# Receptance without the meta tokens, and a first chunk that reads nothing

## The chip, the core and the metric

The program runs on one core of a Trainium2 chip. The metric is the device time of one execution in microseconds (us). Three executions of the kernel before took 1640.95, 1644.88 and 1644.90 us, median 1644.88. The core's engines are TensorE (PE in the profile, PEld for its weight loads), VectorE (DVE), ScalarE (ACT), GpSimd (POOL) and SyncE (SP, which here only issues transfers). They run their own instruction streams and meet at semaphores.

## What is computed

A block of two layers on 16 meta tokens followed by 512 tokens, 1024 features wide. Layer 0 is an attention layer with its feed-forward part, layer 1 an RWKV-7 layer with its own. The output drops the meta tokens. The part that matters here is the recurrence of layer 1:

```python
xs = h[None] + xx[None] * mu[:, None, None, :]
rkv = jnp.einsum('nbtd,nde->nbte', xs[:3], w_rkv)
r, k, v = rkv[0], rkv[1], rkv[2]
...
def step(S, inp):
    r_t, w_t, k_t, v_t, a_t, b_t = inp
    sa = jnp.einsum('bhij,bhj->bhi', S, a_t)
    S = (S * w_t[:, :, None, :] + sa[..., None] * b_t[:, :, None, :]
         + v_t[..., None] * k_t[:, :, None, :])
    return S, jnp.einsum('bhij,bhj->bhi', S, r_t)
...
S0 = jnp.zeros((B, N_HEADS, HEAD_DIM, HEAD_DIM), jnp.float32)
_, y = lax.scan(step, S0, seq_in)
...
bonus = jnp.sum(r_h * k_h * r_k.astype(jnp.float32), axis=-1, keepdims=True) * v_h
...
return rms_norm(h[:, N_META:], final_norm)
```

The receptance r enters nothing but the outputs y and the bonus of its own token. After layer 1 no token looks at another, so y of a meta token reaches no output.

## The kernel before

All large products are in a split form: weight and input are each a high and a low part, and a product is three matmuls (high by high, high by low, low by high; types fp32r). One *unit* is a block of 128 output features. Its weights come by one transfer into w_raw, ScalarE writes w_hi (L125), VectorE writes w_lo (L129), TensorE multiplies, and ScalarE or VectorE evicts. There are two buffers of each kind and two pairs of PSUM banks, used in turn.

The function Front computes the inputs of the recurrence in 32 units. Its tensor() runs them in a written order; each of the 8 receptance units R_UNITS (23, 25 to 31) has 8 row tiles, each in two column halves of 264 (spans, L1914, row_products, L1922), 48 matmuls on line L1928. Between the last five units spread() (L1976, matmuls on L1984) sends the key norms back to all partitions two heads' tiles at a time. VectorE scales the keys with them (L1743, L1747), GpSimd multiplies (L1903), and at the end forms the first chunk's bk (L1909, L1910). evict() (L1552) copies a receptance unit of 528 columns into r.rr on ScalarE. A pad of 48 zero columns ahead makes 576 columns.

chunk_stage then runs the recurrence in 9 chunks of 64 columns over 16 heads; chunk 0 holds the pad and the 16 meta tokens. It is a block of its own: every engine ends Front before any begins it. A step for c does two things interwoven: the *preparation* of chunk n = c + 1 and the *chain* of chunk c. The first step (c = -1) only prepares chunk 0, the second (c = 0) chains chunk 0 and prepares chunk 1. Preparation: l_products (L2437 to L2443), transposes of bk and v (L2452, L2462), a triangular inverse by doubling (times_x L2510, x_times L2529 and L2538, with VectorE between each pair at L2316, L2329, L2339; three levels for chunk 0, five for the others), the quarter products quads (L2476: bk by the pair a, r, 128 stationary by 128 moving columns), which VectorE masks into akm (keys, L2354) and arm (reads, L2358), and a_v (L2488). Chain: w_product (state by a, L2550, woven into the first times_x), chain_u (L2558), y_state_product (state by r, L2563, woven into the second times_x), chain_y (L2569), chain_s (the new state) and the gate's product. products() on VectorE (L2290, L2291) makes ar, and on GpSimd (L2267, L2268) bk of the next chunk; l_products waits for both. bk has one buffer, so GpSimd waits until the quads of the chunk before are done.

The two places where an order is written that matters below:

## Time and profile before

| what | value |
|---|---|
| median of 3 executions | 1644.88 us (1640.95, 1644.88, 1644.90) |
| span of the profiled execution | 1638.5 us |
| TensorE busy | 1567.2 us, 96% of the span |
| VectorE, ScalarE, GpSimd busy | 852.3, 637.0, 156.7 us |
| mean granted TensorE clock | 0.983 |
| the chain that ended last | TensorE on L785 and L1248, 25% of the span |

The profiled execution has no time of its own in the measurements shown, only its span from the first to the last instruction. The median lies 6.4 us above it, which holds what is around the span and the difference between executions. In the profile a matmul's duration is its way through the array, and neighbours overlap, so the pace is read from start to start, not from the duration. A product of fp32 operands (all of chunk_stage but the gate) shows as two matmul records.

### The profile page before, as it was taken

How to read it: one execution, taken by the hardware profiler on the slowest of the kernel's cores; microseconds unless marked ns; L12 is line 12 of the kernel's file. 1: busy time of each engine (PE TensorE's matmuls, PEld its weight loads, DVE VectorE, ACT ScalarE, POOL GpSimd, SP SyncE). 2: the span in 40 equal slices, each digit the busy share in tenths (PEclk: the TensorE clock that was granted, in tenths of full speed). 3: DMA queues.
4: the chain of work that ended last, by engine and by line, in shares of the span. 5: the costliest groups of instructions: out<-in, count | busy, mean ns of one | idle time of the engine just before them, and what ended most of it. 6: DMA issues, size and time to landing. Idle time of an engine off the chain costs nothing. (4 is left out here: it accounts for less than half of the span.)

```text
span 1638.5 us, 35327 instructions
## 1 busy us (share of the span) xinstructions
PE 1567.2 (96%) x15881; PEld 1410.4 (86%) x15881; DVE 852.3 (52%) x1201; ACT 637.0 (39%) x880; POOL 156.7 (10%) x180
## 2 busy tenths in 40 slices
PE   6999998999999999999999989999789999999997
PEld 5998987999999999989988978888558888888886
DVE  5675665544433444677566545545485444344432
ACT  3654654332212223455566333333244322122322
POOL 3100100001000015000000411101010010001100
PEclk9999999999999999998999989999999999999999
DMA  4112121333332333662222100000303333233331
GB/s 132 53 59 72 53 72 46 91 91 90 105 89 78 91 90 115 176 183 71 62 72 59 39 19 4 4 4 5 106 28 98 94 91 114 81 90 102 100 94 64
DMA packets 225814, 126.41 MB, mean 77 GB/s; under 512 B 8856, under 2 KB 220976, under 8 KB 225408
## 3 DMA queue, kind: packets, MB, share of 16 engines
q1 hardware_dynamic: 225360, 124.07, 25.6%
q8 instruction: 125, 2.05, 0.5%
q14 instruction: 25, 0.20, 0.0%
q10 hardware_dynamic: 304, 0.08, 0.0%
HBM read 117.71 MB, written 6.42 MB: 76 GB/s over the span
## 5 line engine op out<-in xcount | busy, mean ns | idle before, releaser
L125 ACT ACTIVATE w_hi<-w_raw 128x1024 fp32r<-128x1024 f32 (+1 forms) x200 | 224.3, 1122 | 548.0 <-PE psg L785 305.8
L785 PE MATMUL psg<-x_hi,w_hi 128*128 128x264 f32 (+1 forms) x1080 | 350.2, 324 | 1.8 <-DVE w_lo L129 1.8
L785 PE MATMUL psg<-x_lo,w_hi 128*128 128x264 f32 (+1 forms) x1080 | 350.4, 324 | 0.0
L785 PE MATMUL psg<-x_hi,w_lo 128*128 128x264 f32 (+1 forms) x1080 | 349.6, 324 | 0.0
L129 DVE TENSOR_TENSOR w_lo<-w_raw,w_hi 128x1024 fp32r<-128x1024 f32 (+1 forms) x200 | 261.9, 1310 | 139.8 <-ACT w_hi L125 139.6
L785 PEld LDWEIGHTS psg<-x_hi,w_hi 128*128 128x128 f32 x1080 | 202.8, 188 | 20.1 <-DVE w_lo L129 2.2
L785 PEld LDWEIGHTS psg<-x_lo,w_hi 128*128 128x128 f32 x1080 | 202.8, 188 | 17.4 <-issue 0.2
L785 PEld LDWEIGHTS psg<-x_hi,w_lo 128*128 128x128 f32 x1080 | 203.3, 188 | 16.7
L1248 PE MATMUL psg<-mid_hi,w_hi 128*128 128x264 f32 (+1 forms) x528 | 170.8, 323 | 2.5 <-DVE w_lo L129 2.5
L1248 PE MATMUL psg<-mid_lo,w_hi 128*128 128x264 f32 (+1 forms) x528 | 170.0, 322 | 0.0
L1248 PE MATMUL psg<-mid_hi,w_lo 128*128 128x264 f32 (+1 forms) x528 | 169.4, 321 | 0.0
L1928 PE MATMUL psg<-x_hi,w_hi 128*128 128x264 f32 x400 | 119.0, 298 | 4.6 <-DVE w_lo L129 2.5
L1928 PE MATMUL psg<-x_lo,w_hi 128*128 128x264 f32 x400 | 116.4, 291 | 0.0
L1928 PE MATMUL psg<-x_hi,w_lo 128*128 128x264 f32 x400 | 116.2, 291 | 0.0
L1172 POOL TENSOR_TENSOR mid_lo<-up,mid_hi 128x528 fp32r<-128x528 f32 (+1 forms) x40 | 52.6, 1315 | 657.7 <-ACT mid_hi L908 657.7
L1248 PEld LDWEIGHTS psg<-mid_hi,w_hi 128*128 128x128 f32 x528 | 99.2, 188 | 11.6 <-DVE w_lo L129 3.6
L1248 PEld LDWEIGHTS psg<-mid_lo,w_hi 128*128 128x128 f32 x528 | 99.2, 188 | 7.8
L1248 PEld LDWEIGHTS psg<-mid_hi,w_lo 128*128 128x128 f32 x528 | 99.3, 188 | 7.6
L958 DVE TENSOR_TENSOR res<-res,psg 128x512 f32<-128x512 f32 (+1 forms) x38 | 26.4, 694 | 143.5 <-PE psg L1248 116.9
L1005 DVE TENSOR_TENSOR gate<-psg,rstd 128x528 f32<-128x528 f32 (+1 forms) x44 | 30.8, 700 | 122.3 <-PE psg L785 115.3
L1015 DVE TENSOR_TENSOR up<-psg,rstd 128x528 f32<-128x528 f32 (+1 forms) x44 | 30.8, 700 | 111.7 <-PE psg L785 111.7
L1928 PEld LDWEIGHTS psg<-x_hi,w_hi 128*128 128x128 f32 x400 | 78.1, 195 | 10.3 <-issue 5.7
(389 smaller groups left out, 3182.7 us busy)
## 6 DMA issues: line engine op xcount, KB each, us to landing
w_raw<-in_w_ffn_in_dram SPq DMA_DIRECT2D x88, 512.0 KB, 3.8
w_raw<-in_w_ffn_out_dram SPq DMA_DIRECT2D x40, 704.0 KB, 4.6
w_raw<-in_w_qkv_dram SPq DMA_DIRECT2D x24, 512.0 KB, 3.8
w_raw<-in_w_rkv_dram SPq DMA_DIRECT2D x24, 512.0 KB, 4.1
w_raw<-in_w_o_attn_dram SPq DMA_DIRECT2D x8, 512.0 KB, 4.1
w_raw<-in_w_o_rwkv_dram SPq DMA_DIRECT2D x8, 512.0 KB, 4.2
v_first<-v_pair SPq DMA_DIRECT2D x8, 264.0 KB, 2.0
res_kept<-res SPq DMA_DIRECT2D x1, 2112.0 KB, 7.8
```

The lines of the kernel that those rows point to most:

```text
L125: k.nc.scalar.activation(k.w_hi[j][:, 0:kt, :], k.raw[j][:, 0:kt, :], ACT.Copy).then_inc(k.hi_ready[j].h, 1)
L129: k.nc.vector.tensor_tensor(k.w_lo[j][:, 0:kt, :], k.raw[j][:, 0:kt, :], k.w_hi[j][:, 0:kt, :].bitcast(F32), ALU.subtract).then_inc(k.lo_r ...
L785: done = k.nc.tensor.matmul(k.psg[:, 2 * j + c, 0:size], w[:, t, :], x, start=t == first and n == 0, stop=t == last and n == 2)
L958: nc.vector.tensor_tensor(row, row, self.psum(i % 2), ALU.add).then_inc(self.freed(i), 1)
L1005: nc.vector.tensor_tensor(self.cols(b.gate), self.psum(0), self.cols(k.rstd), ALU.mult)\
L1015: nc.vector.tensor_tensor(self.cols(b.up), self.psum(1), self.cols(k.rstd), ALU.mult)\
L1172: nc.gpsimd.tensor_tensor(b.mid_lo[:, r, self.t0:T], b.up[:, self.t0:T], b.mid_hi[:, r, self.t0:T].bitcast(F32), ALU.subtract).then_inc(se ...
L1248: done = k.nc.tensor.matmul(self.bank(i, c), w[:, t, :], x, start=t == 0 and n == 0, stop=t == count - 1 and n == 2)
L1928: done = nc.tensor.matmul(k.psg[:, 2 * j + c, 0:size], w[:, t, :], x[:, at:at + size], start=t == 0 and a == 0, stop=t == KT - 1 and a == 2)
```

## The change

Receptance is computed for the 512 tokens alone, so a receptance unit is one piece of 512 columns in one PSUM bank (24 matmuls in place of 48) and is evicted as 512 columns into r.rr from column 64 on. The reads of chunk 0 are left out: no product of ar by r, no arm, no y_state_product, no chain_y, no copy of y; and, since the state is zero there, no w_product: wt is minus av. Chunk 0's quarter products have 64 moving columns (a alone) in place of 128. Semaphore counts shift with it: arm_r now counts chunk 0's keys, y_d, w_d, y_r and ar_r start one chunk later, and chain_s waits for u itself in chunk 0.

```diff
+    def spans(self, n):
+        return [(META, SEQ)] if n >= MIX_R else [(0, HALF), (HALF, HALF)]
...
+        def r_evict(m):
+            i = R_UNITS[m]
+            self.wait_done(act, i)
+            nc.scalar.activation(r.rr[:, m, C:TP], k.psg[:, 2 * ((self.u0 + i) % 2), :], ACT.Copy)\
+                .then_inc(self.freed(i), 1)
...
-        evict(r.rr, R_UNITS, 0)
+        r_evict(0)
...
-        for t in (r.gs, r.aa, r.rr, r.vv, r.kk_in):
+        for t in (r.gs, r.aa, r.vv, r.kk_in):
...
-            at, size = spans[c]
+            at, size = self.spans(n)[c]
...
         def unit(i, first):
             begin(i)
-            for c in range(2):
+            for c in range(len(self.spans(first))):
                 for t in range(KT):
                     row_products(i, first + t, c)
...
                     if chain:
-                        act.wait_ge(y_d.h, c + 1)
-                        nc.scalar.activation(chunk(r.xn, c), wy_ps, ACT.Copy).then_inc(y_r.h, 1)
+                        if c:
+                            act.wait_ge(y_d.h, c)
+                            nc.scalar.activation(chunk(r.xn, c), wy_ps, ACT.Copy).then_inc(y_r.h, 1)
...
                     else:
                         nc.vector.tensor_tensor(ar[p][:, :, 0, :], chunk(r.xn, n), ch.w_ext[:, :, 0:C], ALU.mult)
-                    nc.vector.tensor_tensor(ar[p][:, :, 1, :], chunk(r.rr, n), ch.w_ext[:, :, 1:C + 1],
-                                            ALU.mult).then_inc(ar_r.h, 1)
+                        nc.vector.tensor_tensor(ar[p][:, :, 1, :], chunk(r.rr, n), ch.w_ext[:, :, 1:C + 1],
+                                                ALU.mult).then_inc(ar_r.h, 1)
...
                 def keys(n, half):
                     dve.wait_ge(quad.h, 2 * n + half + 1)
-                    nc.vector.tensor_tensor(akm[C:P, :, :].rearrange("p (b m) c -> p b m c", b=2)[:, :, pairs(half), :],
+                    done = nc.vector.tensor_tensor(akm[C:P, :, :].rearrange("p (b m) c -> p b m c", b=2)[:, :, pairs(half), :],
...
+                    if n == 0:
+                        done.then_inc(arm_r.h, 1)
                 def reads(n, p, half):
+                    if n == 0:
+                        return
...
+                        if c:
+                            dve.wait_ge(w_d.h, c)
+                            nc.vector.scalar_tensor_tensor(wt[:], wy_ps, -1.0, av[q][:], ALU.mult, ALU.subtract)\
+                                .then_inc(wt_r.h, 1)
+                        else:
+                            nc.vector.tensor_scalar(wt[:], av[q][:], -1.0, None, ALU.mult).then_inc(wt_r.h, 1)
...
+                    size = P if n else C
                     for h, m, rows in heads[first:first + len(parts) * KT // 2]:
-                        last = mm(pair_ps[:, h % 2, (m % 4) * P:(m % 4) * P + P],
+                        last = mm(pair_ps[:, h % 2, (m % 4) * P:(m % 4) * P + size],
                                   bk[rows, m, :, :].rearrange("p a c -> p (a c)"),
-                                  ar[p][rows, m, :, :].rearrange("p a c -> p (a c)"), start=True, stop=True)
+                                  ar[p][rows, m, :, :].rearrange("p a c -> p (a c)")[:, 0:size], start=True, stop=True)
...
                 def chain_s(c, q):
+                    if c == 0:
+                        pe.wait_ge(u_r.h, 1)
...
-                    w = (lambda m, rows: w_product(c, q, m, rows)) if chain else None
-                    y_state = (lambda m, rows: y_state_product(c, q, m, rows)) if chain else None
+                    w = (lambda m, rows: w_product(c, q, m, rows)) if c > 0 else None
+                    y_state = (lambda m, rows: y_state_product(c, q, m, rows)) if c > 0 else None
...
-                    if chain:
+                    if c > 0:
                         chain_y(c, q)
```

TensorE at the last spread, in Front, before the change (psg: the unit's sums; psx: the spread):

```order
L1928 MATMUL psg<-x_lo,w_hi0 128x264
L1928 MATMUL psg<-x_hi,w_lo0 128x264
L1984 MATMUL psx<-key_norm_91,put_92 128x264 x4
L1928 MATMUL psg<-x_hi,w_hi1 128x264
L1928 MATMUL psg<-x_lo,w_hi1 128x264
L1928 MATMUL psg<-x_hi,w_lo1 128x264
```

and with it:

```order
L1936 MATMUL psg<-x_lo,w_hi0 128x512
L1936 MATMUL psg<-x_hi,w_lo0 128x512
L1992 MATMUL psx<-key_norm_91,put_92 128x264 x4
L1936 MATMUL psg<-x_hi,w_hi1 128x512
L1936 MATMUL psg<-x_lo,w_hi1 128x512
L1936 MATMUL psg<-x_hi,w_lo1 128x512
```

The spread stands at the same place between two units; the unit behind it has 24 rows of 512 columns in place of 48 of 264.

VectorE in the step that prepares chunk 0, from the first half's keys (akm) on, before (ar1 is chunk 1's, arm0 chunk 0's, g2_lo the gate weight's low part):

```order
L2354 TENSOR_TENSOR akm_10962<-psx,strict 64x2x256
L2316 TENSOR_TENSOR w_raw1<-psg,cross2 128x32x8
L2358 TENSOR_TENSOR arm0_10954<-psx,incl 128x2x256
L2290 TENSOR_TENSOR ar1_10949<-xn_80,w_ext_83 128x8x64
L2291 TENSOR_TENSOR ar1_10949<-rr_79,w_ext_83 128x8x64
L2329 TENSOR_TENSOR xt0_10956<-xt0_10956,psg 128x32x8
L2354 TENSOR_TENSOR akm_10962<-psx,strict 64x2x256
L2358 TENSOR_TENSOR arm0_10954<-psx,incl 128x2x256
L2365 TENSOR_TENSOR g2_lo_99<-g2_raw_98,g2_hi_100 80x2048
```

and with the change:

```order
L2363 TENSOR_TENSOR akm_10769<-psx,strict 64x2x256
L2325 TENSOR_TENSOR w_raw1<-psg,cross2 128x32x8
L2299 TENSOR_TENSOR ar1_10756<-xn_80,w_ext_83 128x8x64
L2300 TENSOR_TENSOR ar1_10756<-rr_79,w_ext_83 128x8x64
L2338 TENSOR_TENSOR xt0_10763<-xt0_10763,psg 128x32x8
L2363 TENSOR_TENSOR akm_10769<-psx,strict 64x2x256
L2378 TENSOR_TENSOR g2_lo_99<-g2_raw_98,g2_hi_100 80x2048
```

Both maskings of arm0 are gone, and all behind them moves up.

TensorE in the step that chains chunk 0, behind the first half of chunk 1's quads, before (xt1 and xs belong to chunk 1's inverse):

```order
L2529 MATMUL psg<-w_raw0,xs_10964 64x32 x2
L2476 MATMUL psx<-ar1_10949,bk_85 128x128 x4
L2510 MATMUL psg<-xt1_10957,low_10963 64x32 x16
L2569 MATMUL psg<-arm0_10954,uv0_10952 64x64 x16
L2529 MATMUL psg<-w_raw1,xs_10964 64x32 x2
L2538 MATMUL psg<-xs_10964,w_raw1 64x32 x2
```

and with the change:

```order
L2545 MATMUL psg<-w_raw0,xs_10771 64x32 x2
L2492 MATMUL psx<-ar1_10756,bk_85 128x128 x4
L2526 MATMUL psg<-xt1_10764,low_10770 64x32 x16
L2545 MATMUL psg<-w_raw1,xs_10771 64x32 x2
L2554 MATMUL psg<-xs_10771,w_raw1 64x32 x2
```

Between times_x and the x_times that needs VectorE's answer to it, chain_y no longer stands.

## Rows read from the trace of the kernel before

**Rows 1.** the page, part 4: the chain that ended last, by engine

```profile
PE 27%; DVE 1%; ACT 0%; issue 0%; DVEq 0%; ACTq 0%
```

**Rows 2.** windows, Front's end, chunk stage: PE, PEld, DVE, ACT, POOL busy, PEclk, DMA

```profile
873.50:942.00 68.50, 66.74 (x469) 62.00 (x468) 34.72 (x34) 29.14 (x38) 16.75 (x10) 0.95 0.16 47
942.00:1130.00 188.00, 170.24 (x5673) 152.66 (x5676) 94.98 (x197) 63.92 (x107) 23.00 (x21) 0.97 0.03 7
```

**Rows 3.** windows of plain products, TensorE alone: 264 columns, then 512

```profile
340.00:440.00 100.00, 100.00 (x824) 1.00 0.32 92
1284.00:1400.00 116.00, 116.00 (x502) 1.00 0.35 101
```

**Rows 4.** timeline of TensorE, last receptance unit: start, us, engine, line

```profile
933.09 2.04 PE L1984 MATMUL psx<-key_norm,put 16*128 16x264 f32 x8
...
935.28 0.28 PE L1928 MATMUL psg<-x_lo,w_hi 128*128 128x264 f32 x1
...
940.91 0.28 PE L1928 MATMUL psg<-x_hi,w_lo 128*128 128x264 f32 x1
...
942.30 0.25 PE L2437 MATMUL psx<-ar,bk 64*64 64x32 f32 x2 [1.11 <-PEq L1255]
```

**Rows 5.** timelines of ScalarE and GpSimd at that unit

```profile
941.23 0.61 ACT L1552 ACTIVATE rr<-psg 128x528 f32<-128x528 f32 x1 [6.59 <-PE psg L1928]
...
935.12 3.47 POOL L1903 TENSOR_TENSOR aa<-aa,xn 128x528 f32<-128x528 f32 x2 [4.56 <-DVE xn L1743]
...
940.25 1.27 POOL L1910 TENSOR_TENSOR bk<-kk_in,w_inv 128x512 f32<-128x512 f32 x1
```

**Rows 6.** timeline of TensorE preparing chunk 0, to chunk 1's l_products

```profile
950.48 1.12 PE L2510 MATMUL psg<-xt,low 64*64 64x32 f32 x32 [0.64 <-DVE xt L2329]
951.53 0.71 PE L2476 MATMUL psx<-ar,bk 64*128 64x128 f32 x8
...
956.75 1.16 PE L2476 MATMUL psx<-ar,bk 64*128 64x128 f32 x16
959.51 1.15 PE L2488 MATMUL psg<-uv,akm 64*64 64x64 f32 x32 [1.59 <-DVE arm L2358]
...
962.78 0.32 PE L2437 MATMUL psx<-ar,bk 64*64 64x32 f32 x2 [2.13 <-issue]
```

**Rows 7.** timelines of VectorE and GpSimd there, GpSimd's last row a chunk later

```profile
958.67 0.69 DVE L2358 TENSOR_TENSOR arm<-psx,incl 128x512 f32<-128x512 f32 x1
959.28 2.28 DVE L2365 TENSOR_TENSOR g_lo<-g_raw,g_hi 80x2048 fp32r<-80x2048 f32 x1
...
958.08 1.27 POOL L2267 TENSOR_TENSOR bk<-aa,w_inv 128x512 f32<-128x512 f32 x1 [12.53 <-PE psx L2476]
959.30 3.38 POOL L2268 TENSOR_TENSOR bk<-kk_in,w_inv 128x512 f32<-128x512 f32 x1
...
985.82 1.28 POOL L2268 TENSOR_TENSOR bk<-kk_in,w_inv 128x512 f32<-128x512 f32 x1
```

**Rows 8.** timelines, chaining chunk 0: TensorE, VectorE; last, TensorE's next chain_y

```profile
972.43 0.47 PE L2563 MATMUL psg<-ar,state 64*64 64x64 f32 x3
...
973.70 0.71 PE L2476 MATMUL psx<-ar,bk 64*128 64x128 f32 x8
...
978.30 1.91 PE L2569 MATMUL psg<-arm,uv 128*64 128x64 f32 x32
980.14 0.32 PE L2529 MATMUL psg<-w_raw,xs 64*64 64x32 f32 x2
...
978.40 0.42 DVE L2316 TENSOR_TENSOR w_raw<-psg,cross 128x256 f32<-128x256 f32 x1 [0.25 <-PE psg L2510]
...
1003.55 1.15 PE L2569 MATMUL psg<-arm,uv 128*64 128x64 f32 x32
```

**Rows 9.** windows of low granted clock in the first chunks, TensorE

```profile
961.60:968.40 6.80, 5.62 (x112) 0.52 0.01 2
978.70:982.10 3.40, 3.40 (x95) 0.54 0.00 0
```

More of the change, by code:

```diff
@@ L1684, in scalar @@
         nc.scalar.activation(r.ghid_hi[:], r.ghid[:], ACT.Copy).then_inc(self.gh_hi.h, 1)
-        evict(r.rr, R_UNITS, 1)
+        r_evict(1)
         self.weights_hi(act, 28)
-        evict(r.rr, R_UNITS, 2)
+        r_evict(2)
         key_scale(2)
@@ L1690, in scalar @@
         self.weights_hi(act, 29)
-        evict(r.rr, R_UNITS, 3)
+        r_evict(3)
         key_scale(4)
@@ L1694, in scalar @@
         self.weights_hi(act, 30)
-        evict(r.rr, R_UNITS, 4)
+        r_evict(4)
         key_scale(6)
@@ L1703, in scalar @@
         nc.scalar.activation(r.ch.w_inv[:], r.gs[:, :, 0:C], ACT.Exp, scale=-DECAY).then_inc(r.ch.exps.h, 1)
-        evict(r.rr, R_UNITS, 5)
-        evict(r.rr, R_UNITS, 6)
-        evict(r.rr, R_UNITS, 7)
+        r_evict(5)
+        r_evict(6)
+        r_evict(7)
     def vector(self, dve):
@@ L1811, in vector @@
         self.weights_lo(dve, 17)
-        dve.wait_ge(self.pads_r.h, 6)
+        dve.wait_ge(self.pads_r.h, 5)
         running(0)
@@ L1859, in vector @@
         dve.wait_ge(r.ch.exps.h, 1)
-        dve.wait_ge(self.pads_r.h, 7)
+        dve.wait_ge(self.pads_r.h, 6)
         dve.wait_ge(self.kk_r.h, 2 * KT)
@@ L1913, in tensor @@
         k, r, nc = self.k, self.r, self.k.nc
-        spans = [(0, HALF), (HALF, HALF)]
         def begin(i):
@@ L1929, in row_products @@
                                         start=t == 0 and a == 0, stop=t == KT - 1 and a == 2)
-            if t == KT - 1 and c == 1:
+            if t == KT - 1 and c == len(self.spans(n)) - 1:
                 done.then_inc(k.unit_done[j].h, 1)
@@ L1943, in unit_by_rows @@
                 self.wait_low(pe, first + t)
-                for c in range(2):
+                for c in range(len(self.spans(first))):
                     row_products(i, first + t, c)
@@ L2353, in keys @@
                     dve.wait_ge(quad.h, 2 * n + half + 1)
-                    nc.vector.tensor_tensor(akm[C:P, :, :].rearrange("p (b m) c -> p b m c", b=2)[:, :, pairs(half), :],
-                                            quad_ps[C:P, :, :, 0:C], masks(ch.strict[C:P, :]), ALU.mult)
+                    done = nc.vector.tensor_tensor(akm[C:P, :, :].rearrange("p (b m) c -> p b m c", b=2)[:, :, pairs(half), :],
+                                                   quad_ps[C:P, :, :, 0:C], masks(ch.strict[C:P, :]), ALU.mult)
+                    if n == 0:
+                        done.then_inc(arm_r.h, 1)
                 def reads(n, p, half):
+                    if n == 0:
+                        return
                     nc.vector.tensor_tensor(arm[p][:].rearrange("p (b m) c -> p b m c", b=2)[:, :, pairs(half), :],
@@ L2372, in step @@
                         dve.wait_ge(av_r.h, c + 1)
-                        dve.wait_ge(w_d.h, c + 1)
-                        nc.vector.scalar_tensor_tensor(wt[:], wy_ps, -1.0, av[q][:], ALU.mult, ALU.subtract)\
-                            .then_inc(wt_r.h, 1)
+                        if c:
[4 more added lines that the diff above has]
+                            nc.vector.tensor_scalar(wt[:], av[q][:], -1.0, None, ALU.mult).then_inc(wt_r.h, 1)
                         if not prep:
@@ L2426, in l_products @@
                     if n:
-                        pe.wait_ge(ar_r.h, n + 1)
+                        pe.wait_ge(ar_r.h, n)
                         pe.wait_ge(bk_r.h, n)
                     if n > 1:
-                        pe.wait_ge(y_r.h, n - 1)
+                        if n > 2:
+                            pe.wait_ge(y_r.h, n - 2)
                         pe.wait_ge(s_step.h, n - 1)
@@ L2468, in quads @@
                     if half == 0 and parts[0] == 0:
-                        if n == 0:
-                            pe.wait_ge(ar_r.h, 1)
                         pe.wait_ge(uvv_r.h, n + 1)
@@ L2545, in begin_w @@
                         if not prep:
-                            pe.wait_ge(y_r.h, c)
+                            pe.wait_ge(y_r.h, c - 1)
                         settle()
@@ L2617, in step @@
                             y_state(m, rows)
-                    if chain:
+                    if c > 0:
                         chain_y(c, q)
```

## The prediction

> **What bounds the kernel now.** I read the page first: TensorE is busy for 96% of the span, and the chain that ended last runs over TensorE [rows 1]. That share is an average, so next come the windows of the two stages that the change touches [rows 2]. At the end of Front TensorE is busy 66.74 of 68.5 us, the others at most 34.72: every column that a receptance unit drops is time. In the chunk stage it is busy 170.24 of 188 us, in short pieces that wait in turn for VectorE; there a removed product counts only where nothing else was late anyway. So the third view is the timeline at the three places where the change cuts, and the fourth the granted clock, which falls to 0.52 and 0.54 of full in two stretches of the first chunks [rows 9].
>
> **Receptance units.** The trace of before has both shapes in plain products, on other lines. With 264 columns 824 matmuls take 100.0 us, 0.1214 us from start to start; with 512 columns 502 take 116.0 us, 0.2311 us [rows 3]. So a piece of 264 costs 27 cycles of 2.4 GHz over its columns and a piece of 512 some 42, and the halved count buys less than half of the overhead. A unit is 48 x 0.1214 = 5.83 us before and 24 x 0.2311 = 5.55 us after, 0.28 less. In the receptance units themselves the pace is 5.63 us over 46 steps, 0.1224 us [rows 4]; if the 512 form does not share this slight lag the unit gives 5.88 - 5.55 = 0.33. I take 0.29 and 8 units: 2.3 us (2.2 to 2.6).
>
> The Trainium skill (TensorE: Matmul & The Clock Gate, Back-to-back issue gap) gives N / 2.4 + 2.5 ns for the isolated gap. By it 264 columns would take 112.5 ns and 512 columns 215.8, a unit would give 48 x 112.5 - 24 x 215.8 = 221 ns, the eight 1.8 us, and the time would be 0.5 us above my forecast. The trace disagrees with both figures (121.4 and 231.1 ns), and I go by the trace.
>
> Does the whole of it reach the end of Front? Only the last unit is in doubt, since a block ends when all engines have ended it. From the start of the last spread at 933.09, ScalarE's eviction ends at 941.84, 8.75 us later; GpSimd's last bk product, which hangs on the spread and not on the unit, ends at 941.52, 8.43 us later [rows 4, 5]. TensorE and the eviction come 0.29 earlier, to 8.46. GpSimd is then level with them, so the last unit counts in full, and nothing beyond it would. The weights of the next unit are no limit: each unit needs one splitting step on ScalarE and one on VectorE, and both engines are free for half of the stage [rows 2]. The eviction of 512 columns in place of 528 and the dropped clearing of the pad of rr are off the path.
>
> **Preparing chunk 0.** Three things go: the product of ar by r, two maskings of 0.69 us (the one at 958.67 is of this kind), and half of the moving columns of the quads. The ar product stood ahead of VectorE's first inverse step, but that step was waiting for GpSimd's clearings, whose count does not change: nothing. The maskings stood behind the step that TensorE wants next: nothing by themselves, except that a_v comes earlier, for which nobody waits. What l_products of chunk 1 wait for, at 962.78, is bk of chunk 1, which ends at 959.30 + 3.38 = 962.68, and GpSimd starts it when the second half of the quads is done, at 958.08 [rows 6, 7]. So only the length of those quads counts. 16 records of 128 columns take 1.16 us, less 0.22 for the last one's way through the array 0.063 us each; the nearest row with 64 moving columns is a_v, 32 records in 1.15 us, 0.030 each [rows 6]. 16 x 0.033 = 0.5 us; at the other end the 128 stationary columns, which stay, could set the pace, and it is 0. I take 0.4 for the quads. The first half of them gives nothing: TensorE is next held by VectorE. GpSimd's second product takes 3.38 us where one chunk on it takes 1.28 [rows 7]: the difference, 2.1, is VectorE's g_lo of 2.28 us beside it. Without the maskings g_lo moves up by about 1.2 us, and still falls wholly within GpSimd's two products: no change. But l_products start at the lower clock [rows 9]. If the clock rises when it did, time won ahead of that is worth half. So the term is 0.3 us (0 to 0.5).
>
> The Trainium skill (TensorE: Matmul & The Clock Gate, LDWEIGHTS) says that a weight load goes by its columns, P / 1.2 ns, whatever the rows: 107 ns for 128 columns. By it these quads would be set by their weights, this term would be 0 and the time 0.3 us higher. The trace has them 63 ns apart, which the rule's figure cannot be; but that the stationary columns do not shrink is the lower bound above.
>
> **Chaining chunk 0.** w_product is woven into the first times_x, and the transposes behind wait for a copy by ScalarE: 0 (at most 0.2, as next). y_state_product is woven into the second: from 972.43 to 973.70 it is 1.27 us, where the same times_x alone takes 951.53 - 950.48 = 1.05 [rows 6, 8]: 0.2 us. chain_y runs from 978.30, and x_times behind it start at 980.14. They need VectorE's masking, 978.40 + 0.42 = 978.82 [rows 8], and 0.15 more for the hand-over, as a_v starts 0.15 after the masking it waits for [rows 6, 7]: 978.97. That is 1.17 us as profiled. But this chain_y ran mostly at the lower clock (1.91 us against 1.15 for the next chunk's [rows 8, 9]). At full clock it takes 1.15 - 0.07 = 1.08 from start to start and bares 0.67 us of waiting: 0.4. The low stretch does not go because chain_y goes; other work will stand in it. So I take 0.6 (0.4 to 1.2). wt from SBUF, the copy of y that is left out and chain_s's own wait for u (which chain_y waited for much earlier in the step) are off the path.
>
> **The sum.** 2.3 + 0.3 + 0.2 + 0.6 = 3.4 us. The profiled span of 1638.5 becomes 1635.1. With the 6.4 us that separate this span from the median of 1644.88, the time is 1641.5 us. By the ends of the terms it lies between 1640.4 and 1642.1, before any change of clock.
>
> **Rivals.** *The clock gives back.* The granted clock fell twice in the first chunks, for 6.8 and 3.4 us [rows 9]; 6.8 us at half the pace cost at most 3.4 us. The three executions lie at 1640.95 and, twice, at 1644.9: 3.9 us apart, about one such stretch. All work behind Front moves by over 2 us, so a stretch may fail to arise: 1641.5 - 3.4 = 1638.1. For it: the median of before is in the upper group. Against: the gaps ahead of 962.78, 1.59 and 2.13 us [rows 6], which seem to bring the first stretch on, do not close.
>
> *The units gain little.* If GpSimd's end or a wait that I do not see takes back the front, only the chunk terms are left: 1644.88 - 1.1 = 1643.8. For it: GpSimd has 0.03 us to spare. Against: it can hold back the last unit alone, and the 512 form's pace is measured over 502 matmuls. That the change does not do what it says is excluded for the shapes by the rows of the program.
>
> *Slower: the thinner chain holds the clock down.* TensorE loses filler work just where it alternates with VectorE: y_state_product, chain_y and half of the quads. Between the two low stretches, from 968.4 to 978.7, the clock was not low. If it stays at half there, these 10.3 us join their neighbours, and with about half of it bound by TensorE it costs 5 us: 1641.5 + 5 = 1646.5. It turns the sign from 7 us more at the lower level on. For it: the idle gap ahead of chunk 1 grows by about a microsecond, since a_v ends earlier. Against: the stage as a whole is at 0.97 of the clock [rows 2], and the removed products were mostly beside others.
>
> **How the numbers follow.** Forecast 0.44, a low stretch fewer 0.30, little gain 0.16, slower 0.10. The likeliest is 1641.5; a clock that differs by half a stretch puts its own range at 1639.8 to 1643. A measurement of this kernel can tell about 0.3%, 4.9 us, from no change: below 1640.0 is faster, above 1649.8 slower. Below lie most of the second case (0.29) and a tenth of the first (0.05): 0.34. Above lies the far end of the last: 0.03. Between: 0.63. The range that should hold it 8 times in 10 takes in most of the second case and two thirds of the fourth: 1637.4 to 1646.
>
> **What would show it.** In the profile after: 24 matmuls of 512 columns in each receptance unit, 0.231 us apart, so 5.55 us a unit; at the end of Front, ScalarE and GpSimd ending within 0.1 us of each other; chunk 0's quads at 0.03 to 0.05 us a record; l_products of chunk 1 waiting for GpSimd's bk still; in chunk 0's chain, a gap of some 0.6 us between times_x and x_times; low-clock stretches as long as before. I am wrong if the 512 form runs at another pace here, if the low stretches in chunks 0 and 1 differ by more than 3 us, or if the chunk stage gains more than 2 us at the same clock.

## The result, and the profile after

The changed kernel takes 1655.36 us (median of 10 executions, 1647.15 to 1664.37), the kernel before 1644.89 beside it (10 executions, 1639.81 to 1651.92). The ratio is 1.0059, interval 1.0034 to 1.0083: slower by 0.6%, where 1641.5 us and "no change, or faster" was forecast. The time lies outside the range. The ratios in this document leave out executions more than 1.5% above the fastest of their kernel, six in all; medians, ranges and clocks keep them.

The profiled execution is the slowest of the ten: 1664.37 us, span 1662.6, mean granted clock 0.960, where before had a span of 1638.5 at 0.983. First the windows that answer to [rows 2], the front's end and the chunk stage, then the stretches of low clock that answer to [rows 9], and the first step of the chunk stage:

```profile
873.50:938.00 64.50, 62.60 (x270) 48.60 (x268) 33.10 (x33) 28.31 (x37) 16.80 (x10) 0.95 0.17 50
942.00:1130.00 188.00, 173.78 (x4759) 156.50 (x4761) 80.35 (x167) 52.85 (x88) 17.10 (x12) 0.78 0.01 3
...
938.20:961.70 23.50, 18.11 (x436) 16.73 (x436) 10.67 (x18) 8.55 (x14) 7.71 (x9) 0.73 0.11 31
948.90:966.00 17.10, 13.64 (x248) 12.86 (x242) 7.58 (x11) 2.32 (x5) 4.55 (x2) 0.50 0.01 3
979.70:996.80 17.10, 17.10 (x328) 15.24 (x325) 6.44 (x13) 2.94 (x6) 2.51 (x2) 0.50 0.01 3
1007.00:1030.90 23.90, 23.90 (x466) 21.57 (x464) 8.58 (x18) 3.53 (x7) 2.51 (x2) 0.50 0.01 3
```

The reader is to see two things. The front's end has the clock of before, 0.95. In the chunk stage the clock is 0.78 in place of 0.97, and in the same 188 us TensorE has 4759 matmul records in place of 5673 (96 fewer are the change itself) while it is busy for *longer*, 173.78 us against 170.24: for 82 of these 188 us it runs at 1.2 GHz, half of 2.4. The busy share alone would have shown nothing.

By stage, read from start to start: the chunk stage begins at 938.2 in place of 942.3 (4.1 us won, 2.5 of them ahead of Front's first product, in code that the change doesn't touch, and 1.6 in Front, which has 30.7 us of low clock in place of 27.3), lasts 257.2 us from its first l_products to its last chain_y in place of 233.4 (23.8 lost), and what is behind it takes 467.2 in place of 462.8 (4.4 lost). The clock was low for 82.7 us of the stage, before for 16.3. The 66.4 us more at 1.2 GHz cost these 23.8 us and the one or so that the change wins in this stage, about 25 in all: 0.37 us for each. They lie in chunk 0's preparation, in the step behind it, and in chunks whose code the change does not touch.

The places of the forecast, on TensorE (answers to [rows 4, 6, 8]):

```profile
931.55 0.40 PE L1936 MATMUL psg<-x_lo,w_hi 128*128 128x512 f32 x1
...
936.67 0.39 PE L1936 MATMUL psg<-x_hi,w_lo 128*128 128x512 f32 x1
938.19 0.25 PE L2454 MATMUL psx<-ar,bk 64*64 64x32 f32 x2 [1.13 <-PEq L1255]
...
947.48 0.66 PE L2492 MATMUL psx<-ar,bk 64*128 64x64 f32 x8
...
950.50 1.92 PE L2526 MATMUL psg<-xt,low 64*64 64x32 f32 x32
953.04 1.92 PE L2545 MATMUL psg<-w_raw,xs 64*64 64x32 f32 x32 [0.62 <-DVE w_raw L2325]
954.89 1.97 PE L2492 MATMUL psx<-ar,bk 64*128 64x64 f32 x16
957.75 1.97 PE L2504 MATMUL psg<-uv,akm 64*64 64x64 f32 x32 [0.89 <-DVE akm L2363]
961.67 0.32 PE L2454 MATMUL psx<-ar,bk 64*64 64x32 f32 x2 [1.95 <-issue]
...
975.93 0.25 PE L2545 MATMUL psg<-w_raw,xs 64*64 64x32 f32 x2 [0.61 <-DVE w_raw L2325]
979.42 1.35 PE L2526 MATMUL psg<-xt,low 64*64 64x32 f32 x24 [1.31 <-issue]
```

And on ScalarE, then GpSimd, at the front's end and at chunk 1's bk (answers to [rows 5, 7]):

```profile
937.09 0.60 ACT L1568 ACTIVATE rr<-psg 128x512 f32<-128x512 f32 x1 [6.02 <-PE psg L1936]
...
936.43 1.27 POOL L1920 TENSOR_TENSOR bk<-kk_in,w_inv 128x512 f32<-128x512 f32 x1
...
957.02 1.27 POOL L2276 TENSOR_TENSOR bk<-aa,w_inv 128x512 f32<-128x512 f32 x1 [15.58 <-PE psx L2492]
958.24 3.33 POOL L2277 TENSOR_TENSOR bk<-kk_in,w_inv 128x512 f32<-128x512 f32 x1
```

From 950.50 every product of chunk 0's preparation takes 1.92 to 1.97 us where [rows 6] have 1.12 to 1.16: the clock had fallen at 948.9. In before it fell at 961.3, when that preparation was over and l_products alone were left for it.

### The profile page after: what moved, and what is told of

It reads as the page before. It is cut to its first block and busy times, and to the rows that moved or that the text cites. A ratio compares the mean times of both kernels' runs of the same rounds, so it can differ in the third digit from the quotient of the medians.

```text
span 1662.6 us, 34743 instructions
## 1 busy us (share of the span) xinstructions
PE 1592.9 (96%) x15593; PEld 1424.1 (86%) x15593; DVE 849.2 (51%) x1198; ACT 636.1 (38%) x879; POOL 157.2 (9%) x179
## 5 line engine op out<-in xcount | busy, mean ns | idle before, releaser
L785 PE MATMUL psg<-x_hi,w_hi 128*128 128x264 f32 (+1 forms) x1080 | 350.9, 325 | 1.8 <-DVE w_lo L129 1.8
L785 PE MATMUL psg<-x_lo,w_hi 128*128 128x264 f32 (+1 forms) x1080 | 351.0, 325 | 0.0
L785 PE MATMUL psg<-x_hi,w_lo 128*128 128x264 f32 (+1 forms) x1080 | 350.2, 324 | 0.0
L785 PEld LDWEIGHTS psg<-x_hi,w_hi 128*128 128x128 f32 x1080 | 203.1, 188 | 20.3 <-DVE w_lo L129 2.2
L785 PEld LDWEIGHTS psg<-x_hi,w_lo 128*128 128x128 f32 x1080 | 203.7, 189 | 16.9
L1936 PE MATMUL psg<-x_hi,w_hi 128*128 128x264 f32 (+1 forms) x336 | 107.2, 319 | 4.6 <-DVE w_lo L129 2.5
L1936 PE MATMUL psg<-x_lo,w_hi 128*128 128x264 f32 (+1 forms) x336 | 104.6, 311 | 0.0
L1936 PE MATMUL psg<-x_hi,w_lo 128*128 128x264 f32 (+1 forms) x336 | 104.3, 310 | 0.0
L1936 PEld LDWEIGHTS psg<-x_hi,w_hi 128*128 128x128 f32 x336 | 65.1, 194 | 13.1 <-issue 5.7
```

Source lines behind the costliest of these rows:

```text
L785: done = k.nc.tensor.matmul(k.psg[:, 2 * j + c, 0:size], w[:, t, :], x, start=t == first and n == 0, stop=t == last and n == 2)
L1936: done = nc.tensor.matmul(k.psg[:, 2 * j + c, 0:size], w[:, t, :], x[:, at:at + size], start=t == 0 and a == 0, stop=t == KT - 1 and a == 2)
```

## The experiments

"Filler" is a matmul whose result nobody reads. The columns are the median (executions) and its range, the ratio to before on the same chip with its interval, the mean granted clock of a kernel's executions, and the time that a straight line through all executions (one slope for all kernels, 12 us for 0.01 of clock, scatter 2.3 us) gives it at a clock of 0.980. Before is the 122 executions that ran beside the variants and have a clock (mean 1644.5); its medians there, in four groups, are 1642.50 (beside front_only, chunk_only, fill_chain, fill_gap), 1644.25 (the pads), 1645.23 (fill_prep, the delays, after_quads128) and 1641.94 (the rest). For 12 executions the standard error is some 0.0014 in the mean clock and 0.7 us in the last column, so two variants that differ by 0.002 or 0.003 of clock are not told apart.

```
kernel           median us  (n)   range              ratio   interval         clock   at .980
before, all      1642.73  (122)   1635.98-1658.63    1                        .9795   1644.0
changed kernel   1655.36   (10)   1647.15-1664.37    1.0059  1.0034 to 1.0083  .9688   1642.1
after_again      1656.29    (6)   1649.87-1658.02    1.0070  1.0043 to 1.0097  .9683   1640.8
front_only       1648.70   (12)   1636.35-1658.07    1.0030  1.0000 to 1.0060  .9740   1641.8
chunk_only       1648.71   (12)   1637.59-1660.57    1.0015  0.9983 to 1.0047  .9747   1641.1
fill_chain       1646.87   (12)   1639.29-1661.02    1.0033  1.0010 to 1.0056  .9751   1642.0
fill_gap         1647.79   (12)   1641.33-1662.51    1.0036  1.0011 to 1.0061  .9728   1640.6
after_quads128   1643.86   (12)   1633.48-1665.43    0.9970  0.9941 to 0.9998  .9751   1640.2
fill_prep        1636.26   (12)   1629.87-1647.40    0.9947  0.9918 to 0.9976  .9824   1639.9
fill_early       1643.77   (12)   1629.91-1654.49    1.0005  0.9980 to 1.0030  .9741   1637.1
fill_second      1636.77   (12)   1628.12-1648.72    0.9962  0.9937 to 0.9986  .9823   1640.8
before_fill      1648.46   (12)   1636.64-1656.95    1.0019  0.9992 to 1.0047  .9780   1644.1
after_delay      1650.23   (12)   1639.30-1664.02    1.0015  0.9982 to 1.0048  .9717   1640.1
before_delay     1648.01   (12)   1640.26-1665.58    1.0001  0.9972 to 1.0031  .9753   1643.3
before_pad128    1661.57   (12)   1649.45-1680.67    1.0075  1.0046 to 1.0103  .9766   1657.4
before_pad190    1672.04    (6)   1662.71-1682.96    1.0149  1.0110 to 1.0188  .9788   1670.9
after_pad66      1647.06   (12)   1641.24-1661.34    1.0018  0.9991 to 1.0045  .9753   1643.0
after_pad130     1662.48    (6)   1657.97-1675.03    1.0100  1.0062 to 1.0138  .9727   1655.3
```

Three theories stood against each other. *Thinner work*: TensorE lost products in the stage where it alternates with VectorE, and the clock falls there. *Start*: the stage begins after a front that is 2 us shorter, so what the clock sees ahead of it differs. *Fetches*: TensorE has fewer instructions, so its waits for instruction fetches fall elsewhere. In the expectations C is the fetches, B and later E are the start, and the other letters are thinner work in one place or another.

### Each half of the change alone

front_only is before with the receptance units in one piece of 512 columns; chunk_only is the changed kernel with them in halves again:

```diff
     def spans(self, n):
-        return [(META, SEQ)] if n >= MIX_R else [(0, HALF), (HALF, HALF)]
+        return [(0, HALF), (HALF, HALF)]
...
-        r_evict(0)
+        evict(r.rr, R_UNITS, 0)
```

> Only the receptance units in one piece of 512 columns (and their eviction); the chunk stage is that of before. Theory A (the thinned chunk 0 lets the granted clock fall, and it stays low for longer in the chunks behind): the kernel gains its 2 to 3 us at the clock of before, 1641 to 1643, mean clock as before's. Theory B (it is the front: the shorter units shift the chunk stage or its instruction stream, and that brings on the low clock): 1650 to 1656, mean clock 0.97.

> Only chunk 0 without reads and with quarter products of 64 columns; the receptance units are those of before, in halves of 264. Theory A: 1653 to 1659, mean clock 0.97, long low stretches in the chunk stage. Theory B: 1643 to 1645, clock as before's.

Both theories missed: both kernels lie between the times that A and B gave. At equal clock each half is ahead of before, by 2.2 us (the forecast had 2.3 for the units) and by 2.9 (the forecast had 1.1 for chunk 0). Each also lowers the mean clock, from .9795 to .974 and .975, about three standard errors each, and so neither is faster; together they come to .969. In the profiles the first fall in the stage comes at 14.3 us (front_only) and 15.3 us (chunk_only) after its first l_products, in the changed kernel at 10.7, in before at 19.0. The first row is front_only's, the second chunk_only's:

```profile
960.50:974.20 13.70, 10.80 (x199) 9.86 (x197) 6.30 (x10) 2.69 (x5) 4.61 (x2) 0.50 0.01 2
```

```profile
957.50:967.70 10.20, 7.37 (x142) 6.93 (x139) 4.66 (x5) 1.83 (x4) 4.55 (x2) 0.50 0.01 2
```

So there are two contributions, of similar size. A theory with thinner work alone fails on front_only, whose chunk stage is that of before, and one with the start alone fails on chunk_only, whose front is.

### The changed kernel once more

> The changed kernel unchanged, beside the variants on their chip. Theory D: 1650 to 1656, mean clock 0.969 to 0.974, a fall 10.8 us after the chunk stage begins. Rival (the first ten executions of it drew a bad chip or hour): 1640 to 1645, clock 0.980.

Same time, same clock, and the same first two stretches, at 10.8 and 41.5 us after the stage's start (before's lie at 19.0 and 36.1). The third lies elsewhere, at 147.3, where the first profile has 68.8 and 154.1: the early ones belong to the kernel, the late ones vary from execution to execution.

```profile
949.90:967.00 17.10, 13.65 (x243) 12.86 (x237) 7.72 (x11) 2.21 (x5) 4.55 (x2) 0.50 0.01 3
980.60:1001.10 20.50, 20.50 (x399) 18.20 (x398) 7.37 (x15) 3.96 (x7) 2.50 (x2) 0.50 0.01 3
1086.40:1110.30 23.90, 23.90 (x477) 21.31 (x476) 8.50 (x18) 4.57 (x8) 2.50 (x2) 0.50 0.01 3
```

### Fillers where chain products went, and in the gap

fill_chain gives TensorE matmuls in place of w_product, y_state_product and chain_y of chunk 0; fill_gap gives it ten of 512 columns behind a_v(0), where it waits for chunk 1's bk:

```diff
+                    if c == 0:
+                        w = lambda m, rows: mm(wy_ps[rows, m, :], ar[q][rows, m, 0, :], ch.state[rows, m, :], ...)
...
+                        for h, m, rows in heads:
+                            mm(wy_ps[rows, m, :], uv[q][:, at(h), :], uv[q][:, at(h), :], start=False, ...)
```

```diff
                         a_v(n, p)
+                        if n == 0:
+                            pe.wait_ge(g_hi.h, 1)
+                            for _ in range(10):
+                                mm(k.psg[:, 2, :], r.g_hi[:, 0, 0, :], r.ghid_hi[:, 0, META:T], start=True, ...)
```

> The changed kernel, with TensorE's products of chunk 0's chain put back as fillers that nobody waits for (w_product and y_state_product on the zero state, chain_y's place filled by products of u by u; results unread). TensorE is as dense as before in chunk 0's chain; VectorE, ScalarE and the quarter products stay as changed. Theory A in the form that the removed chain products matter: back to 1642 to 1646. Theory A in the form that the preparation (quarter products, VectorE's maskings) matters, and theory B: stays at 1652 to 1658.

> The changed kernel, with ten filler matmuls of 512 columns on TensorE (unread, into a free bank) between chunk 0's a_v and chunk 1's l_products, where TensorE idled 1.95 us in the profile of after. If the idle gap seeds the low stretches that follow, the time falls to 1640 to 1648 and the mean clock rises to 0.98; if they arise anew in each chunk, or from chunk 0's earlier part, it stays at 1652 to 1658.

Both are better than the changed kernel (1646.87 and 1647.79 against 1655.36) and neither is as good as before. In both the clock still falls 10.8 to 10.9 us into the stage, for 17.1 and 20.5 us, since they fill behind that point. What fill_chain takes away is the second stretch, at 41.5. There the changed kernel waits 0.61 us for VectorE at 975.93, where chain_y stood, and 1.31 us for an instruction at 979.42, and the clock falls at 979.7. In fill_chain that issue wait lies 9 us later. So this run changed a filler and a fetch at once, and does not tell them apart. fill_gap speaks for the fetch: it leaves chunk 0's chain as the change made it, with the wait of 0.61 us, but its issue wait lies 17 us later, and it has no stretch there either.

### Fetches moved by padding

The trace shows instruction transfers of 16 KB, 40 of them in the 197 us from 938 on. That they are TensorE's is inferred: it has some 9500 instructions in 188 us of this stage, 250 to a transfer. Semaphore increments at the start of TensorE's program shift all that follows against those pieces; no other instruction changes:

```diff
         mm = nc.tensor.matmul
+        pad = k.sem("pe_pad")
+        for _ in range(66):
+            pe.sem_inc(pad.h, 1)
```

before_pad190 and before_pad128 do the same to before, with 190 and 128; after_pad66 and after_pad130 to the changed kernel.

> The kernel before with 190 one-word semaphore increments put at the start of TensorE's program, where TensorE waits for the first inputs anyway; nothing else differs. The changed kernel's TensorE program is 578 instructions shorter ahead of the second chunk, and the instruction transfers in the trace carry 256 instructions each, so 190 more bring the chunk stage to the same place in those blocks as in the changed kernel. Theory C (the place of the chunk stage's instructions in the blocks moves TensorE's fetch waits, and with them the granted clock): 1650 to 1657, mean clock 0.970. Theory A (the thinned chunk 0) and theory B (the shorter units as such): 1642 to 1645, mean clock 0.980.

> The same with 128 increments: the place in the blocks that the variant with the receptance units alone has. Theory C: some other time than before, near that variant's 1649 with a clock of 0.974. Theories A and B: 1642 to 1645, clock 0.980.

> The changed kernel with 66 increments at the start of TensorE's program, so that the later chunks lie in the blocks of 256 as in the kernel before. Theory C: mean clock back to 0.980 and 1641 to 1644. Theories A and B: 1653 to 1658 as the changed kernel, clock 0.969.

> The changed kernel with 130 increments, a place in the blocks that no other variant has. Theory C: a time that may differ from both by several us, between 1642 and 1658, with the clock that goes with it. Theories A and B: 1653 to 1658, clock 0.969.

The times are spoilt by something I had not foreseen: the increments cost time themselves. TensorE's first product comes at 3.0 us without them, at 11.1 with 66, 20.5 with 128 and 30.0 with 190, so each takes about 0.15 us. At equal clock 66 cost 1 to 2 us of the whole time, 128 cost 13 and 190 cost 27. The clocks can be read all the same. Before keeps its clock, .9788 with 190 and .9766 with 128: where the fetches lie is not what takes it from .9795 to .969. For the smaller loss of front_only (.9740), whose fetches before_pad128 copies, two clocks of 12 executions that differ by .0026 can't exclude a part for them. The changed kernel rises from .9688 to .9753 with 66 and .9727 with 130. In both profiles the issue wait lies 9 to 14 us later, and there is no stretch at 41.5; the first, at 10.8, stays:

```profile
955.80:972.90 17.10, 13.65 (x241) 12.86 (x235) 7.67 (x11) 2.22 (x5) 4.54 (x2) 0.50 0.01 3
986.50:1007.00 20.50, 18.50 (x655) 16.52 (x649) 10.61 (x23) 7.67 (x13) 2.50 (x2) 1.00 0.02 4
```

These rows are after_pad66's; the second is the place of after_again's 980.60:1001.10, with 655 matmuls in the same 20.5 us in place of 399. So the second stretch goes with a fetch wait close behind VectorE's, and the first does not. The lost clock that 66 and 130 give back is 61% and 36% of the whole. That the second stretch is what they give back is not shown: the later stretches change from execution to execution as well.

The pads show one thing more. With 128 and 190 increments before's stage begins 14.8 and 22.7 us later, and the first fall stays at 19.2 and 18.8 us behind that start; with 66 and 130 the changed kernel's begins 6.8 and 16.9 us later, and its fall stays at 10.8. So the time since the program's start is not what decides it.

### Fillers in chunk 0's preparation

This goes at the first stretch. fill_prep adds 20 fillers of 512 columns to the changed kernel, at five places, from 3 us after the stage's start to the wait for chunk 1's bk:

```diff
+                def fill(n, count, at_bank):
+                    if n == 0:
+                        for _ in range(count):
+                            mm(k.psg[:, at_bank, :], r.ghid_hi[:, 0, 0:P], r.ghid_hi[:, 0, META:T], start=True, ...)
...
                         turn_bk(n)
+                        fill(n, 5, 0)
...
                         x_times(n, 0)
+                        fill(n, 2, 3)
...
                         times_x(n, p, 2)
+                        fill(n, 2, 3)
...
                             quads(n, p, 1)
+                            fill(n, 3, 3)
...
                         a_v(n, p)
+                        fill(n, 8, 3)
```

> The changed kernel with 20 filler matmuls of 512 columns (unread) on TensorE in the waits of chunk 0's preparation: 5 behind the transposes of bk, 2 behind the first x_times, 2 behind the third times_x, 3 ahead of a_v, 8 ahead of chunk 1's l_products. In the profiles so far every kernel with both parts of the change goes to the lower clock 10.7 to 10.9 us after the chunk stage begins, for 17.1 us or more; before does so at 19.0 for 6.8. Theory D (chunk 0's preparation leaves TensorE too idle, and where the fall comes depends on that and on the time the stage begins): the long stretch is gone, first step near 20.5 us in place of 23.5, time 1640 to 1648, mean clock 0.977 or more. Rival (the low stretches of the later chunks are what costs, at random): first step shorter, the time still 1650 to 1656.

1636.26 us: 19 us less than the changed kernel, and 0.53% faster than before (0.24 to 0.82%). The clock is .9824. Both early stretches are gone; in the profile 3.4 us of the whole chunk stage are low, and the first two steps take 20.5 and 22.7 us where the changed kernel takes 23.5 and 30.7. The first steps, and the stage:

```profile
944.60:965.10 20.50, 19.62 (x452) 16.41 (x452) 10.71 (x18) 8.59 (x14) 7.74 (x9) 1.00 0.13 35
...
942.00:1130.00 188.00, 175.00 (x5655) 155.31 (x5653) 93.45 (x195) 64.34 (x107) 25.07 (x23) 0.99 0.03 7
```

and four places of the changed kernel's TensorE timeline, here at the full clock:

```profile
959.21 1.11 PE L2498 MATMUL psx<-ar,bk 64*128 64x64 f32 x16
...
962.29 2.11 PE L2443 MATMUL psg<-ghid_hi 80*128 80x512 f32 x8
965.15 0.25 PE L2460 MATMUL psx<-ar,bk 64*64 64x32 f32 x2 [0.75 <-issue]
977.50 0.25 PE L2551 MATMUL psg<-w_raw,xs 64*64 64x32 f32 x2 [0.61 <-DVE w_raw L2325]
```

The wait of 0.61 us where chain_y stood is there unchanged, and the clock does not fall at it. So the second stretch isn't brought on by that wait alone: here the next issue wait comes 5.7 us behind it, at 983.24, in place of 3.5, is 0.63 us long in place of 1.31, and no stretch went ahead.

fill_early has only the first nine of the 20; before_fill has all 20 in the kernel before; fill_second adds ten more to fill_prep, in the front's second(A2), 55 us earlier, where every profile but chunk_only's had a low stretch:

```diff
+                if which == 2:
+                    for _ in range(3 if m == 0 else 1):
+                        nc.tensor.matmul(k.psg[:, 2 * j, :], k.w_hi[j][0:rank, m, :], r.hid_hi[0:rank, META:T], ...)
```

> The changed kernel with the first 9 of the 20 fillers (behind the transposes of bk, the first x_times and the third times_x). Ten fillers behind a_v alone did nothing: the clock had fallen before them. Theory D in the form that the first 11 us decide: no fall at 10.8, though one may still come at the idle stretch ahead of chunk 1; 1640 to 1647, clock 0.976 to 0.981. Rival (all waits must be filled): 1650 and more.

> The kernel before with the same 20 filler matmuls in chunk 0's preparation as the filled variant of the changed kernel. If the fillers keep the clock up whatever the rest is: 1638 to 1641, clock 0.982, and the change as such is then worth the 2 to 4 us that the filled variants differ by. Rival (the fillers only cure what the change brought): 1643 to 1646, clock 0.980.

> The filled variant with 10 more fillers in Front's last second() (before the a gate's products), ahead of the low stretch of 6.8 to 10.2 us that every kernel but one shows 54 to 58 us before the chunk stage. If that stretch comes from the waits there: it is gone, another 2 to 3 us off, 1633 to 1635. Rival (it comes from elsewhere, or ScalarE is the limit there): 1636 to 1638.

With nine fillers the clock falls 17.6 us into the stage in place of 10.7, and the time is 1643.77, clock .9741: it takes both groups, since the last place alone (fill_gap) did not do it either. In before the fillers win nothing (1.0019, 0.9992 to 1.0047): its fall at 19.0 us stays, the second stretch lasts 23.9 us in this profile, and at equal clock the time is that of before. So fill_prep's gain is not one that before could have had by the same fillers; it takes the change and the fillers. In fill_second the low stretch 55 us ahead of the stage is gone, and nothing further is won. Its profile (1647.44 us, one of its two longest) has no early stretch in the stage and still 47.8 us of low clock in it, from 57.0 and 217.4 us on.

### The moving columns of the quads

after_quads128 gives chunk 0's quads their 128 moving columns back, the second 64 of them zero. TensorE's work there is that of before again:

```diff
                     if n == 0:
+                        nc.vector.memset(ar[p][:, :, 1, :], 0.0)
...
-                    size = P if n else C
+                    size = P
```

> The changed kernel with chunk 0's quarter products on 128 moving columns again (the read half is zero and unread). Theory D in the form that these products' columns keep the clock up: the fall comes 3 us or more later than 10.8 us after the stage's start, and the time is 1648 to 1652. Rival: fall at 10.8 for 17.1 as before, 1653 to 1657.

The mean is 9.6 us below the changed kernel's (median 11.5; the standard error of the difference is 3), the clock .9751, and the first fall comes at 14.3 us in place of 10.8, for 20.5 us. With all twelve executions the mean is that of before beside it (1646.1 and 1646.0). So giving the removed half of the quads back, which the forecast valued at 0.4 us of gain, gives back about half of the lost clock. But taking back either half of the change, fill_chain or 66 increments give back as much (.9740 to .9753), and the edit also adds a clearing on VectorE and a wait for it: that the columns do it is likely from the first fall, and not shown by the time.

### The start of the stage moved

after_delay puts 9 fillers (2.1 us) behind the last receptance unit, so that the changed kernel's stage starts when before's would; before_delay puts 6 (1.4 us) there in before.

```diff
         unit(R_UNITS[7], MIX_R)
+        self.wait_freed(pe, R_UNITS[6])
+        for _ in range(9):
+            nc.tensor.matmul(k.psg[:, 2 * ((self.u0 + R_UNITS[6]) % 2), :], r.ghid_hi[:, 0, 0:P], ...)
```

> The changed kernel with 9 filler matmuls (2.1 us) behind the last receptance unit, which puts the chunk stage back to about the time behind Front's earlier events that it had before. Theory E (it is the time at which the chunk stage begins): the fall comes at 15.3 us after the start for 10.2 us, as in the variant with chunk 0's part alone, and the time is 1646 to 1651 although 2.1 us of work are added. Rival (only what is computed matters): fall at 10.8 for 17.1, and 1656 to 1659.

> The kernel before with 6 filler matmuls (1.4 us) behind the last receptance unit. Theory E: the stage's start is moved against the chip's decisions like in the variant with the shorter units alone, the fall comes near 14.3 us after the start for 13.7 us, and the time is 1648 to 1651, mean clock 0.975. Rival: fall at 19.0 for 6.8, time 1645 to 1646.5, clock 0.980.

Neither settles the theory of the start. after_delay has .9717, between the two kernels, and its profile falls 6.0 us into the stage, earlier than any other, where theory E had 15.3. before_delay falls at 14.6, like front_only, as E said, and has .9753 against .9786 beside it, two standard errors; its time can't be told from before's (1.0001). That the place of the first fall depends on how far the stage lies behind Front's earlier work is supported by this and by front_only; the pads, which move both together, leave it alone. By which rule is open.

## Why the prediction was wrong

*Receptance units: right.* 22 steps of the 512-column form take 936.67 - 931.55 = 5.12 us, 0.2327 each; 24 are 5.58 us, against 5.88 before: 0.29 a unit, the value taken. From the front's first product to the stage, front_only takes 229.63 us and before 231.84, with 27.3 us of low clock in both: 2.2 us, where 2.3 was forecast. In the changed kernel's own profiles it takes 230.26 and 231.52, with 30.7 and 34.1 us of low clock: there the clock already takes back a part of it in Front. The eviction ends at 937.69 and GpSimd's bk at 937.70, level as foreseen.

*Chunk 0's quads: mis-sized.* At full clock, in fill_prep, 16 records take 1.11 us in place of 1.16: 0.05 us and not 0.4. The end of the range at which the 128 stationary columns set the pace was the right one. TensorE's weight loads of these quads, before and then in fill_prep, take the same time with 128 and with 64 moving columns; the third row is the transposes of bk in the changed kernel, which have 128 stationary columns too:

```profile
956.75 0.97 PEld L2476 LDWEIGHTS psx<-ar,bk 64*128 64x128 f32 x16
```

```profile
959.21 0.97 PEld L2498 LDWEIGHTS psx<-ar,bk 64*128 64x128 f32 x16
```

```profile
940.20 1.09 PE L2469 MATMUL psx<-ident,bk 128*128 128x128 f32 x8
```

This is also what the Trainium skill (TensorE: Matmul & The Clock Gate, LDWEIGHTS) makes of it, and its figure of 107 ns is met. The prediction divided by 16 and took 63 ns a record, "which the rule's figure cannot be". But the records start two at a time, some 7 ns apart, and less the last one's 0.19 us the eight pairs come 0.11 us apart, as the eight single records of the transposes do.

*The chain: the wait was right.* TensorE waits 0.61 us where chain_y stood; 0.67 was worked out. What the wait leaves as gain, and the 0.2 us of y_state_product, no run shows singly.

*The sum: about right, at equal clock.* 1642.1 (the first ten executions) and 1640.8 (after_again) against 1644.0: 1.9 and 3.2 us won, forecast 3.4. The sign is safe, since every variant of the changed kernel without costly padding lies below every one of before; the size is not. fill_early, which only adds work to the changed kernel, lies 4.5 us below it at equal clock, so the mean clock does not carry all that differs.

*The clock: this step failed.* The forecast said "low-clock stretches as long as before", and gave 0.03 to a slower kernel. The stretches of the chunk stage sum to 82.7 and 61.4 us in the two profiles, before to 16.3. At 12 us for 0.01 of mean clock, .9795 - .9688 is 13 us, and that less the gain is the result.

*The rival "the thinner chain holds the clock down"* had the right kind of cause. Its place was wrong: it put the loss between the two stretches in chunk 0's chain, while the first fall moves back into chunk 0's *preparation*, 8 us earlier, and stays for 17.1 us in place of 6.8. Its price, 5 us, counted those few microseconds alone and not stretches of 17 to 27 us in later chunks. And it was given 0.10 by an argument that doesn't hold: that the stage stood at 0.97 [rows 2] said that before was well off, not that it was far from the edge. The row that should have counted is [rows 9]: a clock that already falls there for 6.8 and 3.4 us.

Of the causes, shown are: the clock carries the loss (one slope of time against clock fits all kernels to 2.3 us, and at equal clock the changed one is ahead); each half of the change lowers it; filler work in chunk 0's preparation restores it and makes the kernel faster than both. Supported only: that the quads' columns count, and that a fetch wait brings on the second stretch. A rival stands against every finer division of the loss. Nine variants of the changed kernel or of a half of it (both halves, fill_chain, fill_gap, fill_early, after_quads128, after_delay, both pads) all lie at .9717 to .9753, whatever they alter, and none has the stretch at 41.5 us or an issue wait so close behind VectorE's. So a part of the change's loss may belong to the exact place of the fetches in this one kernel, which nearly any edit moves. Only fill_prep and fill_second stand clear above them. Not settled are why a shorter front lowers it, and why later chunks, whose code is that of before, have long stretches in some executions and not in others. A plain reading is that a stretch begun early is followed by others, since fill_prep has 3.4 us of them in its profile; but fill_chain and after_pad130 have the first and few behind it (21.5 and 23.9 us in the stage), and fill_second has none early and 47.8 us later.

The change with its 20 fillers, fill_prep, is the best of all kernels here, level with fill_second: 1636.26 us.

## What to carry to other kernels

In a stage where TensorE alternates with another engine and the granted clock already dips for a few microseconds, price each product that is taken away there twice: what it frees, and what it may cost in clock; here the dips of before (16.3 us) were the smallest and not the largest loss. Compare variants by mean clock and time at equal clock over ten or more executions; a median alone mixes a mechanism of 2 or 3 us with a clock loss of 13. Before a change of clock is put down to one edit, see what an edit with no meaning, such as a few idle instructions, does to it. If the clock is what was lost, put unread matmuls of many columns into the waits ahead of the fall, where TensorE would sit idle anyway, and see whether the two together win.

## What was not expected of the hardware

More work on TensorE made a kernel faster: 20 matmuls of 512 columns, about 4.6 us of work by [rows 3], most of it in waits, took 19 us off. The busy share ahead of the first fall does not tell the kernels apart: in the first 10.7 us of the stage before and the changed kernel are alike, 8.8 us busy, and then one clock falls and the other stays up for 8 us more. Here are the two, before first:

```profile
942.30:953.00 10.70, 8.84 (x302) 8.11 (x305) 4.67 (x10) 6.92 (x11) 3.17 (x7) 1.00 0.22 64
```

```profile
938.20:948.90 10.70, 8.77 (x298) 8.05 (x300) 3.68 (x9) 6.84 (x11) 3.16 (x7) 1.00 0.24 64
```

Halving the moving columns of matmuls with 128 stationary ones saved 0.05 us of 1.16, and undoing it brought the mean down by 9.6 us through the clock, as several other edits did. Semaphore increments at the head of TensorE's stream take about 0.15 us each (first product at 3.0, 11.1, 20.5 and 30.0 us with none, 66, 128 and 190). And waits that the profile gives no reason for ("issue"), 0.5 to 1.3 us in the small matmuls of the changed kernel's stage, move with the count of instructions ahead of them, so that an edit at one place moves a wait at another; that they are waits for instruction fetches is inferred from this.
